# Modulation vectors of the first block, fetched and summed by column quarters between the blocks of the first projection

## The reference, cut to what matters

```python
silu_c = jax.nn.silu(c)
silu_cc = jax.nn.silu(c_ctx)
mod_l = silu_c @ w_mod[l] + b_mod[l]          # 1024 -> 3072: shift, scale, gate
mod_c = silu_cc @ w_mod[l] + b_mod[l]
h_l = rmsnorm(x, norm_g[l]) * (1 + sc_l[:, None]) + sh_l[:, None]
h_c = rmsnorm(ctx, norm_g[l]) * (1 + sc_c) + sh_c
f_in, f_gate, q_a, kv_a, k_pe, m_gate = split_cols(h_lat @ w_in, EVEN_SPLITS)
```

## Time and profile before

| what | us |
|---|---|
| median of 3 executions | 1326.5 (1326.5 to 1328.35) |
| profiled execution, its own time | 1324.11 |
| profiled execution, span of the trace | 1322.3 |
| PE busy | 1276.3 (97%) |
| DVE busy | 933.9 (71%) |
| ACT busy | 522.5 (40%) |
| first product of `fin` | 31.87 |
| end of `fin` | 57.8 |

### The profile page before, as it was taken

One profiled execution on the slowest core, in us unless ns is written; L12 is line 12 of the kernel. 1 busy time (PEld: TensorE's weight loads), 2 busy tenths in 40 slices (PEclk: granted clock), 3 DMA queues, 4 the chain that ended last, 5 costly groups with the idle time before them and its releaser, 6 DMA issues.

```text
span 1322.3 us, 18840 instructions
## 1 busy us (share of the span) xinstructions
PE 1276.3 (97%) x7793; PEld 1059.0 (80%) x7793; DVE 933.9 (71%) x1239; ACT 522.5 (40%) x805; POOL 107.9 (8%) x152
## 2 busy tenths in 40 slices
PE   5999999999999999999999999999999999999996
PEld 2798756448965479889988898987998998899895
DVE  5867687658768665777898666676587789654557
ACT  3322146214346043553344434334354434443432
POOL 2201110100000110011002000001011100000000
PEclk9999999999999999999999999999999999999999
DMA  9743550416620584677973776536567794355551
GB/s 372 243 139 106 180 188 1 150 45 237 206 80 1 187 273 155 241 281 272 314 276 131 252 250 249 191 128 255 187 238 264 276 332 170 127 190 182 184 185 56
DMA packets 104910, 257.75 MB, mean 195 GB/s; under 512 B 8213, under 2 KB 11766, under 8 KB 104570
## 3 DMA queue, kind: packets, MB, share of 16 engines
q1 hardware_dynamic: 80872, 172.40, 38.1%
q0 software_dynamic: 20192, 75.58, 15.9%
q10 hardware_dynamic: 3762, 8.57, 1.8%
HBM read 255.49 MB, written 1.05 MB: 194 GB/s over the span
## 4 chain that ended last, share of the span: by engine, by line
PE 82%; DVE 9%; ACT 4%; DMA 2%; issue 2%; POOL 1%; POOLq 0%; ACTq 0%; DVEq 0%
PE bank L823 80%; PE bank L990 3%; DVE weights_low L2327 1%; DMA start_ring<-in_w_mod_dram 1%; ACT odd_prob L1919 1%; DVE negated_maxima L2572 1%; DVE modulation_sums L2182 1%; ACT weights_high L1726 1%; ACT even_A L1860 1%; DMA even_yT<-in_w_mod_dram 1%; DVE even_A L2279 1%; DVE statistics L2294 0%; DVE x L2293 0%; DVE xn L2287 0%; DMA weight_ring<-in_w_in_dram 0%
## 5 line engine op out<-in xcount | busy, mean ns | idle before, releaser
L2327 DVE TENSOR_TENSOR weights_low<-weight_ring,weights_high 128x2048 fp32r<-128x2048 f32 (+1 forms) x120 | 261.8, 2184 | 202.0 <-ACT weights_high L1726 201.6
L1726 ACT ACTIVATE weights_high<-weight_ring 128x2048 fp32r<-128x2048 f32 (+1 forms) x120 | 219.7, 1831 | 316.2 <-PE bank L823 297.6
L823 PE MATMUL bank<-uT_high,weights_high 128*128 128x256 f32 (+1 forms) x1136 | 324.0, 285 | 0.2
L823 PE MATMUL bank<-uT_high,weights_low 128*128 128x256 f32 (+1 forms) x1136 | 321.3, 283 | 0.0
L823 PE MATMUL bank<-uT_low,weights_high 128*128 128x256 f32 (+1 forms) x1136 | 321.3, 283 | 0.0
L823 PEld LDWEIGHTS bank<-uT_high,weights_high 128*128 128x128 f32 (+1 forms) x1136 | 216.1, 190 | 2.9 <-issue 1.0
L823 PEld LDWEIGHTS bank<-uT_low,weights_high 128*128 128x128 f32 (+1 forms) x1136 | 216.2, 190 | 1.2
L823 PEld LDWEIGHTS bank<-uT_high,weights_low 128*128 128x128 f32 (+1 forms) x1136 | 216.2, 190 | 0.5
L2182 DVE SCALAR_TENSOR_TENSOR modulation_sums<-modulation_ring,silu_c_columns,modulation_sums 128x1024 f32<-128x1024 f32 x112 | 143.7, 1283 | 12.8 <-DMA modulation_ring<-in_w_mod_dram 5.4
L823 PE MATMUL bank<-weights_high,hidden_high 128*128 128x512 f32 x256 | 100.2, 391 | 0.2 <-DVE weights_low L2327 0.2
L823 PE MATMUL bank<-weights_low,hidden_high 128*128 128x512 f32 x256 | 99.8, 390 | 0.0
(11 more groups left out here) (337 smaller groups left out, 2195.5 us busy)
## 6 DMA issues: line engine op xcount, KB each, us to landing
weight_ring<-in_w_in_dram SPq DMA_DIRECT2D x52, 1024.0 KB, 5.8
modulation_ring<-in_w_ada_dram POOLq DMA_DIRECT2D x48, 1024.0 KB, 6.3
weight_ring<-in_w_down_dram SPq DMA_DIRECT2D x32, 1024.0 KB, 4.8
weight_ring<-in_w_up_dram SPq DMA_DIRECT2D x28, 1024.0 KB, 5.2
modulation_ring<-in_w_mod_dram POOLq DMA_DIRECT2D x16, 1024.0 KB, 5.6
weight_ring<-in_o_w_in_dram SPq DMA_DIRECT2D x10, 1024.0 KB, 5.0
norm_rows<-in_w_branch_dram SPq DMA_DIRECT2D x16, 512.0 KB, 5.8
weight_ring<-in_w_o_dram SPq DMA_DIRECT2D x8, 1024.0 KB, 7.9
```

Source lines behind the costliest of these rows:

```text
L823: return track(pe.matmul(*args, **kw))
L1726: act.activation(ring[:, s, c0:kn * cols], wring[:, slot, c0:kn * cols], ACT.Copy).then_inc(S["high_ready"], 1)
L2327: dve.tensor_tensor(lo[:, s, c0:kn * cols], wring[:, slot, c0:kn * cols], hi[:, s, c0:kn * cols].bitcast(F32), ALU.subtract).then_inc(w_fr ...
```

## The change

The eight chunks of `w_mod` are cut the other way. A chunk is now all eight k's by 256 columns, still 1 MB, and the order is shift and scale of the first quarter of the columns, then of the second, and so on (four parts of two chunks). POOL issues parts 0 and 1 at the start, and parts 2 and 3 after chunk 1. A part has one bank for the rows of shift and scale side by side, and one for its columns. After a part, the two blocks k = 2p and 2p + 1 can be modulated. On PE, part 0 comes ahead of `fin`, part 1 behind k = 0, part 2 behind k = 2, part 3 behind k = 3; a part is its rows, two transposed blocks and its quarters. The fillers become 4 products ahead of the transposes and 6 ahead of `fin`.

ACT modulates straight out of the transpose's bank; DVE's eight copies are gone. `x` and `ctx` have a semaphore each; DVE takes the statistics of `x` ahead of the small vectors, norms the latents, then takes one context tile while ACT squares the other. SP issues `fin` 0 in two halves of two k's right behind `ctx`, without waiting; `fin` 1 waits for chunk 3, `fgate` 0 for chunk 7. High and low parts of `fin` 0 are made in two halves as well (`high_first`, `low_first`).

The diff, cut to its core (jobs and semaphore counts are left out):

```diff
-START_ORDER = [(c, 2 * h + q) for h in range(2) for c in range(PE_MODS) for q in range(2)]
+START_PARTS = 4
+START_COLS = D // START_PARTS
+START_ORDER = [(c, q) for q in range(START_PARTS) for c in range(PE_MODS)]
...
-            for n, (name, h) in enumerate(FIRST_SLABS):
-                if n < 3:
-                    sp.wait_ge(s_full[(1, 5, 7)[n]], 16)
+            first, _, _ = w_slab("fin", 0, None)
+            view = w_view(sec, "fin", 0)
+            for k, landed in ((0, fin_in), (2, w_full[sec.slab(("fin", 0))[0]])):
+                sp.dma_start(view[:, k:k + 2, :], first[:, k:k + 2, :]).then_inc(landed, 16)
+            for n, (name, h) in enumerate(FIRST_SLABS[1:]):
+                if n < 2:
+                    sp.wait_ge(s_full[(3, 7)[n]], 16)
                 load(sec, name, h)
...
-            inverse_root(1, 0, TALL)
-            pool.wait_ge(s_full[2], 16)
-            start_chunks(1)
+            pool.wait_ge(S["latent_var"], 1)
+            pool.tensor_tensor(root[:, 0, 0:TC], nwt[:, 0, 0:TC], root[:, 1, 0:TC], ALU.pow
+                               ).then_inc(S["latent_root"], 1)
+            inverse_root(1, TC, TC)
+            pool.wait_ge(s_full[1], 16)
+            start_chunks((2, 3))
+            b, n = sec.bank(("start rows", 2), 1)
+            pool.wait_ge(full[b], n)
             pool.wait_ge(s_full[7], 16)
...
+            def start_rows(part):
+
+                o = start(("start rows", part))
+                for n, (c, q) in enumerate(START_ORDER):
+                    if q != part:
+                        continue
                     pe.wait_ge(s_full[n], 16)
+                    w = startw[n].rearrange("p (k n) -> p k n", k=KD)
+                    for k in range(KD):
+                        r = 32 * (k % 4)
+                        ins = product(o[r:r + 32, START_COLS * c:START_COLS * c + START_COLS], cpad[:, k, :], w[:, k, :],
+                                      start=(c == 0 and k < 4), stop=(k >= 4), skip_group_check=True)
...
+            def start_part(part):
+
+                start_rows(part)
+                turn_x("xT", xn_e, (2 * part, 2 * part + 1), TALL)
+                add_quarters(part)
+
+            fin = [start(("fin", m)) for m in range(4)]
+            start_rows(0)
+            keep_busy(fin[0], 4)
+            turn_x("xT", xn_e, (0, 1), TALL)
+            add_quarters(0)
...
-            keep_busy(fin[0], 3)
+            keep_busy(fin[0], 6)
             for half in range(2):
-                w = slab("fin", half)
+                if half == 0:
+                    pe.wait_ge(S["fin_low"], 1)
+                    w = in_place_view("fin", 0)
+                else:
+                    start_part(3)
+                    w = slab("fin", 1)
                 for k in range(4):
+                    if half == 0 and k == 2:
+                        slab("fin", 0)
                     h_e_ready(4 * half + k)
...
-                    if half == 0 and k == 0:
-                        start_rows(6, 7)
-                        add_quarters(0, 1)
-                    if half == 0 and k == 1:
-                        add_quarters(1, 1)
+                    if half == 0 and k in (0, 2):
+                        start_part(1 + k // 2)
...
+            for part in range(START_PARTS):
+                copy_rows(part)
+                if part == 0:
+                    high_first(0)
+                if part == 2:
+                    high_e("fin", 1)
+                copied(("start columns", part))
+                for k in (2 * part, 2 * part + 1):
+                    o = ready(("xT", k))
                     for v in range(2):
-                        w = whole_e[:, k, N * v:N * v + N]
-                        ins = act.activation(w, w, ACT.Identity, bias=mcol[:, 0, v * KD + k:v * KD + k + 1],
+                        ins = act.activation(whole_e[:, k, N * v:N * v + N], o[:, N * v:N * v + N], ACT.Identity,
+                                             bias=mcol[:, 0, v * KD + k:v * KD + k + 1],
                                              scale=mcol[:, 1, v * KD + k:v * KD + k + 1])
-                    ins.then_inc(S["h_whole"], 1)
-                    if k == 1:
-                        copy_rows(0, 1)
+                    release(ins, ("xT", k))
+                if part == 0:
+                    high_first(1)
...
+            for part in range(START_PARTS):
+                start_columns(part)
+                if part == 0:
+                    low_first(0)
+                if part == 2:
+                    low_e("fin", 1)
+                    b, n = sec.bank(("start rows", 3), 1)
+                    dve.wait_ge(full[b], n)
+                for k in (2 * part, 2 * part + 1):
+                    split_h(k)
+                if part == 0:
+                    low_first(1)
```

More of the change, by code:

```diff
@@ L112, in first_jobs @@
     jobs = [(("vec",), last)]
[L113 to L117 removed]
+    for q in range(START_PARTS):
+        jobs += [(("start rows", q), (0,)), (("start columns", q), (0,))]
+        jobs += [(("xT", k), (1, 2, 3)) for k in (2 * q, 2 * q + 1)]
+    jobs += [(("fin", m), hi) for m in range(4)]
     jobs += [(("fgate", m), lo) for m in range(4)]
@@ new lines, in add_quarters @@
+            def add_quarters(part):
+                copied(("start rows", part))
+                o = start(("start columns", part))
+                for c in range(PE_MODS):
+                    for k in range(2):
+                        n0 = START_COLS * part + P * k
+                        ins = product(o[:, 4 * c + 2 * k:4 * c + 2 * k + 2], modrow[:, c, n0:n0 + P], quarters,
+                                      start=True, stop=True)
+                done(ins, ("start columns", part))
@@ new lines, in _, with copy_rows, high_first @@
+            act.activation(xn_e[:, TALL - 1, :], x[:, TALL - 1, :], ACT.Square, accum_out=csquare[:, 1:2]
+                           ).then_inc(S["ctx_squares"], 1)
+            def copy_rows(part):
+                o = ready(("start rows", part))
+                c0 = START_COLS * part
+                copy_out(("start rows", part), modrow[:, :, c0:c0 + START_COLS],
+                         o[:, :].rearrange("p (c n) -> p c n", c=PE_MODS))
+            def high_first(piece):
+                half = 2 * COLS
+                slot, before = sec.slab(("fin", 0))
+                act.wait_ge(w_full[slot] if piece else fin_in, 16)
+                c = slice(half * piece, half * piece + half)
+                act.activation(whigh_e[:, 0, c], wring[:, slot, c], ACT.Copy
+                               ).then_inc(S["even_high"] if piece else S["fin_high"], 1)
```

165 lines of the change are left out of this document (65 added, 100 removed).

## The result

| kernel | median of 15, us | lowest to highest |
|---|---|---|
| before | 1327.42 | 1325.32 to 1329.53 |
| after | 1332.57 | 1327.71 to 1335.89 |

The ratio is 1.004, with a 95% interval of 1.0029 to 1.005: slower by 5.2 us. I had forecast 1328.5 and a range up to 1332.0; the time lies 0.6 us above it, and "slower", to which I gave 0.33, came true. It is the longest of the 15, 3.3 us above the median, so what its trace shows is on the long side. Its mean granted clock is 0.991, against 0.996 before.

What follows compares the result with a forecast made beforehand. PE, busy for 97% of the span, bounds the kernel. `fin` starts 6.4 us earlier but ends 1.6 later; with a 0.4 us wait that is +2.0 on 1326.5, so 1328.5 us, range 1324.3 to 1332.0.

Steps and rivals of the forecast that it cites:

- Step 1: Kernel start, until part 0 can start: chunk 1 lands at 16.2 us (bounds 15.4 to 18.0).
- Step 2: From chunk 1 to `fin`: clock rises at 19.5 us, `fin` starts at 25.5, 6.4 us earlier than 31.87.
- rival (a): At the start, clock rises at 22.4 instead of 19.5, `fin` starts 1.45 us later: 1330.0 us; chance 0.17.
- Step 3: Inside `fin`: 7.65 us more work, 0.35 us wait; `fin` ends at 59.35, 1.6 us later than 57.74.
- rival (c): Row products of 256 columns miss their columns' pace, +2 us per part: 1334.5 us; (c) and others slower 0.06.
- rival (b): At the start, POOL's queue slow on 1 KB rows, `fin` 2 to 4 us later: 1330.5 to 1332.5; chance 0.10.
- Step 4: Behind `fin`: DVE 3 us later, PE waits 0.4 us at `qa` 1, then the delay dies out; sum +2.0 us.
- last sign of error: Whole kernel: the forecast is wrong if the time moves by more than the end of `fin` does.

Runs made afterwards that it cites:

- late_slab: after, with SP issuing the first slab of `fin` only when chunk 1 has landed; 1332.77 us, ratio to before 1.0032.
- warm: after with five fillers between chunk 0 and chunk 1; 1333.85 us, ratio to before 1.0036.
- wide_warm: after with five fillers between chunks 0 and 1, and column products streaming 48 columns instead of 1; 1328.82 us.
- fill_warm: fill_after with five fillers between chunk 0 and chunk 1; 1327.49 us, ratio to before 0.9991.
- wide_before2: wide_before measured once more, unchanged; 1325.76 us, ratio to before 0.9991.
- fill_before: wide_before with three fillers in PE's 2.00 us wait near 374 us; 1325.13 us, ratio to before 0.9984.
- fill_after: wide_after with three fillers in PE's 2.00 us wait near 374 us; 1329.83 us, ratio to before 1.0012.
- wide_after: after, with the products that turn sums into columns streaming 48 columns instead of 1; 1331.07 us.
- after2: after measured once more, unchanged; 1333.39 us, ratio to before 1.0048.
- fill_early: fill_after with parts 2 and 3 one block of `fin` earlier; 1327.98 us, ratio to before 0.9996.
- shift: before with 14 more fillers ahead of `fin` (17 for 3); 1336.16 us, ratio to before 1.0062.
- wide_shift: wide_before with 7 more fillers ahead of `fin` (10 for 3); 1328.16 us.
- wide_before: before, with the products that turn sums into columns streaming 48 columns instead of 1; 1325.94 us.
- wide_best: wide_after with five fillers between chunks 0 and 1, none behind chunk 1, slab's second half after chunk 1, parts 2 and 3 one block earlier; 1327.35 us.

## Why the prediction was wrong

**Step 1** was nearly right. Chunk 1 was there at 16.83, inside 15.4 to 18.0, where I took 16.2. late_slab shows the cause that I named: without SP's slab beside it the chunk was there at 15.59.

**Step 2** is one of two terms that failed. I let the clock rise at 19.5; it rose near 22.3. This is rival (a), with its mechanism and nearly its time (22.4): PE stood still for 2.42 us behind chunk 0, and the higher level came later. That the wait matters is shown by the edits that shorten it. In the seven profiles with the start of after, `fin` started at 26.20 to 27.45; with fillers in the wait (warm, wide_warm, fill_warm) it started at 25.11 to 26.11. That the profiled execution hit 22.3 is luck in part, since the seven differ. And I had read the rise in one profile of before as if the instructions ahead of it fixed its time. In the profile of wide_before2, with the same start as before, the fourth chunk and most of the first transposes still ran at the lower level, and `fin` started at 31.89 all the same:

```profile
20.94 1.94 PE L823 MATMUL bank<-start_ring,even_E 128*32 128x512 f32 x8 [1.12 <-DMA start_ring<-in_w_mod_dram]
22.80 2.62 PE L990 MATMUL bank<-constants,even_A 128*128 128x128 f32 x16
...
31.89 0.58 PE L823 MATMUL bank<-even_hT_high,even_weights_high 128*128 128x512 f32 x1
```

Before, the start hangs on the landing of chunks, and the waits for them absorb most of a late rise (in the profile of fill_before it came later still, and `fin` started at 32.47). In after, the chain from chunk 1 to `fin` is PE's work without slack, and a late rise is paid in full. The Trainium skill, "TensorE: Matmul & The Clock Gate", section "What's actually happening", says that the chip's watch over the engine does not restart with the kernel, so that the rise varies from run to run. The traces agree: the same ten records of filler behind chunk 0 took 3.17 us in `warm` and 4.41 in fill_warm. `fin` started 1.6 us later than I said (27.09 for 25.5): 0.6 from chunk 1, 1.0 from the clock. fill_warm puts the clock's share of the median at 2.3 to 2.8 us. That is more than 1.0, and I can only argue why: an earlier start also leaves DVE with less of a backlog (the last split ends at 53.1 us there, at 53.8 in fill_after), and fill_after's own profile already started `fin` at 26.80.

**Step 3** was right. A part costs 33.62 - 29.90 = 3.7 us (3.77 predicted; 29.90 is the last product's start, 29.67, and its 0.23 us), `fin` with all three takes 60.78 - 27.09 = 33.7 us from its first product to its end (59.35 - 25.5 = 33.85 predicted), and the wait ahead of k = 2 is 0.2 (0.35). The row products of 256 columns run at the pace of their columns, 32 records in 1.93 us, which rules out rival (c). Chunks 2 to 7 were there when PE wanted them, and chunk 1 at 16.83 instead of 18 to 20, which rules out rival (b). Its premise was a misreading: the transfer of 7.3 us in the earlier trace rows did have much beside it. From 18 to 26 us, the eight us behind its issue, SP's queue moved 1.05 MB and POOL's, with earlier chunks ahead of it, 2.29 MB, so its rows of 2 KB need not have cost anything. The range left out (c) rightly; that it ended 0.6 us short comes from steps 2 and 4 failing together, which I had priced one at a time.

**Step 4** is the other term that failed. I had seen the backlog (the last split at 52.5; it ended at 54.1, of which 1.4 is PE's own delay), the place (`qa` 1) and its thin slack, and priced the wait at 0.4 us. It was 2.0 in the profiled execution, 0.7 and 0.6 in the traces of wide_after and fill_after, and nothing in that of after2. What I missed is between the two: DVE's sums wait for their weights. POOL issues the next chunk only when DVE frees a slot, which is now 5.5 us later, and that transfer took 9.1 us (5.5 before); DVE stood still for 2.09 us (0.39 before, at a later sum). So DVE came to `qa` 1 later by 6.9 us, not by some 3 as in my sum. The idle time in which I let the delay die out comes only behind that slab. And by the medians of fill_early the backlog costs 1.9 to 2.1 us, more than the wait in the trace of fill_after (0.6), which that edit takes away. So it seems to cost elsewhere too, but where is shown only in part: in the traces of fill_before and fill_after PE's distance grows from 3.1 to 4.0 us between 697 and 885 us, where PE waits for low parts on DVE (0.2 us before, 0.8 after).

With the two terms at their sizes in the trace (the end of `fin` 1.4 later than I said, the waits 1.6 longer) the sum is 2.0 + 1.4 + 1.6 = 5.0 us, beside 5.2 in the medians. That it comes so close is partly luck: the trace is of a long execution, and at 110 us its distance is 5.5, of which 0.5 was not traced. The traces of after2, wide_after and fill_after stand only 2.9 to 3.6 us behind before's 110.13 there. In a usual execution, then, more of the loss comes behind 110 us than this sum says.

**What the sum did not contain at all** is the clock behind 110 us. "The change is worth what it moves the end of `fin`, and nothing else, unless it makes PE wait later" is false for this kernel: a delay of 5.85 us cost 9.0 without any other change (with the interval and the clocks given above), and the changed kernel lost 5.2 us where the end of `fin` moved by 3.0, which is the last sign of error that I had named. For the changed kernel that share is 6.0 less 4.7, 1.3 us, in the one comparison that splits it on one chip; the first pair of comparisons (5.2 as it is, 5.1 held) gives nearly nothing. The estimate from the mean clocks speaks for 1.3, but the interval of after2's ratio alone is 2.9 us to either side. The share stays open; the two comparisons give 0.1 and 1.3 us.

## What to carry to other kernels

An earlier first product is worth nothing by itself where the engine is the bound: the question is which idle time of PE disappears, and here the head start was PE's own work, done later. Where work of the bounding engine replaces waits at a cold start, its speed there becomes part of the critical path; here filler in the wait ahead of the last chunk gained 2.2 to 2.8 us where the clock behind it was held, and dropping the four behind that chunk cost nothing. Before costing small changes of a kernel that is as long as PE's work, look in several profiles for stretches in which the granted clock falls. Here they were products of one column, which could stream 48 in the same time, and a wait of 2.00 us ahead of such products, which filler could cover.

## What the runs showed of the hardware

- The granted clock fell while PE was busy without a gap. With 3.5 us of products of one column by 128 columns of weights the rows show 0.77 and 0.83 for 150 to 160 us in `shift` and in after, and 1.00 in wide_shift, whose products stream 48 columns in the same time (1.88 against 1.84 us for sixteen records). It still fell once behind the wide ones (0.83 in wide_before).
- The code alone does not fix whether it falls. The profiles of wide_before and wide_before2, one kernel, show 0.83 and 1.00 from 150 to 160 us; those of after and after2 show 1.00 and 0.84 from 380 to 390. Before had no fall near 150 us in its one profile, and the same products 1.4 to 5.8 us later had one in all six profiles; whether the time decides it or chance, no run here shows. The spread of a kernel's times follows: 13 us for before over 35 runs (1324.48 to 1337.3), 4 us for fill_before over 12.
- A gap of 2.00 us followed by products of 48 columns had the same effect in four of eight profiles (0.82 and 0.66 from 370 to 390 us in wide_best); with three fillers in the gap it was 1.00 in five of five.
- Rows of 1 KB did not slow POOL's queue: from 20 to 26 us it moved 2.43 MB, 0.41 MB a microsecond, in 627 packets of 3.9 KB, so the packets were larger than the rows. Beside SP's slab, from 14 to 15 us, the two queues shared the engines. They moved as many packets, but POOL's were twice as large (packets, megabytes and share of the engines' time in that microsecond):

```profile
q0 software_dynamic: 62, 0.25, 64.6%
q1 hardware_dynamic: 63, 0.13, 35.9%
```
